# Conditioning matmuls of a hybrid decoder step: four units share one K tile, and one set of transposes per vector

## The chip, the cores and the metric

The kernel runs on one core of one Trainium2 chip. The metric is the time of one execution on the device in microseconds (us), as the median over runs; lower is better. In the profile PE is TensorE (PEld its weight loads), ACT is ScalarE, DVE is VectorE, POOL is GpSimd and SP is SyncE, which issues the transfers.

## The reference, cut to what matters

One step of a two-layer decoder trunk for 256 prompt tokens and 8 sequences of 4 tokens, 288 columns in all, at model width 2048. Layer 0 mixes with a causal convolution of 31 taps and a gated linear attention, layer 1 with a spatial gating unit and windowed attention; each has an input projection, an output projection and a SwiGLU block. All sub-layers are modulated by a conditioning vector, and that part the change touches:

```python
def adaln(c, w, b):
    return jnp.split(jax.nn.silu(c) @ w + b, 6, axis=-1)     # c: 9 rows of 2048, w: 2048 x 12288 for each layer

def modulate(x, g, shift, scale):
    return rms_norm(x, g) * (1.0 + scale[:, None, :]) + shift[:, None, :]

mp = adaln(c_prompt, w_ada[layer], b_ada[layer])             # shift, scale, gate of the mixer; the same of the FFN
hp = modulate(yp, g_mix[layer], mp[0], mp[1])
yp = yp + mp[2][:, None, :] * (op @ w_out[layer])
yp = swiglu_sublayer(yp, mp[3], mp[4], mp[5], ...)
```

So there are 12 vectors of 2048 entries (6 for each layer), each for 9 conditioning rows, and their weights are 192 MB of float32, read once.

## The kernel before

**The projections.** All activations lie with the model dimension on the partitions. A weight step is a tile of 2048 KB (`raw`, two slots, the projections and the gate/up matrices `gu`) or of 1408 KB (the down matrices, `down`). ACT rounds it to `w_hi` (L868), DVE subtracts to get `w_lo` (L1191), and PE multiplies hi by hi, lo by hi and hi by lo (L556 to L558): 48 matmuls of 288 columns for half a step, 33 for half a `down` step. A *body* is two steps, four halves. SP loads a step when the tile two steps before has been split. Semaphores order all of it.

**The conditioning work.** The 12 x 2048 columns are cut in 48 *units* of 512 columns. The weights of a unit come in four *slots* of 1024 KB, each holding four K tiles of 128 rows with 512 columns. The first 8 units (`PRE`) run at the start, before anything else can, from the four slots that `raw` gives (`load_pre`, L391); the others ride in the bodies of layer 0 with a ring `aring` of two slots (`load_ada`, L383): one unit per body. For a slot PE issues four matmuls, one into each group of 32 output columns of the array (L572): group j takes K tile 4s+j. So after four slots the four groups each hold a partial sum over four K tiles. ACT copies the bank to `adarow` (`ada_copy`, L936); PE multiplies it by `sel`, a matrix of stacked identities, four times (`ada_turn`, L582), which sums the four groups and turns the result; DVE adds the bias into `mods` (`ada_bias`, L1289). In a body the slots stand so: slot 0 after the first half, slot 1 after the second, slots 2 and 3 after the third, the turn after the fourth.

**Order of the stages.** Start (units 0 to 7), norm of x, `zr`, `gate` (4 bodies, units 8 to 11), `zconv` (4, units 12 to 15), `z` (2, units 16 and 17), the mixer `mix0`, `out` (4, units 18 to 21), norm, `gu` (11, units 22 to 32), `down` (8, units 33 to 40), `gu` (11, the first 7 with units 41 to 47), `down` (8, without units), norm; then layer 1, which has no conditioning work. Bodies of one kind run in a loop on each engine (`Fori`), with addresses from registers; the first and the last body of a segment are partly written out (`peel`).

**The convolution.** In `gate` and `zconv` DVE runs two instructions for each of 31 taps and each of 8 tiles (`conv`, L1278 and L1280) between its splits. It reads 30 history rows, which SP loads (L472, eight transfers in runs of 120 bytes) after the norm has released the memory; at the end of the first norm DVE waits for that history, and the next split of weights stands behind that wait:

```python
                    norm(norms, final=norms == 4)
                    norms += 1
                    if norms == 1:
                        dve.wait_ge(history_landed, 16 * CT)
                        dve.wait_ge(history_zero, 1)
```

SP issues the history (L472) before the weights of the second `gate` step and the first slots of unit 8.

**mix0** waits until the new convolution state has been stored (L413, eight transfers in runs of 120 bytes), which SP issues after the last load of `z`.

Of the kernel before, what the change touches and what calls it, by code (L numbers as in the profile page):

```python
# [63 lines left out]
class Seg:  # L64


    def __init__(self, kind, layer, bodies, m, first, unit=None, group=0):
        self.kind, self.layer, self.bodies, self.m = kind, layer, bodies, m
        self.first = first
        self.unit = unit  # L70
# [11 lines left out]
def plan():  # L82
    segs, norm = [], "norm"
    segs += [Seg("zr", 0, 1, 1, 0), Seg("gate", 0, 4, 2, 0, 8), Seg("zconv", 0, 4, 2, 8, 12, 0),
             Seg("z", 0, 2, 2, 16, 16, 16)]
    segs += ["mix0", Seg("out", 0, 4, 2, 0, 18), norm]
    for layer in range(2):
        if layer:
            segs += [Seg("kv", 1, 1, 1, 0), Seg("q", 1, 2, 2, 1), Seg("sgu", 1, 4, 2, 5), "mix1",
                     Seg("out", 1, 4, 2, 0), norm]  # L90
        segs += [Seg("gu", layer, 11, 2, 0, None if layer else 22),
                 Seg("down", layer, 8, 2, 0, None if layer else 33, 0)]
        if layer:
            segs += [Seg("gu", 1, 11, 2, 22)]
        else:
            segs += [Seg("gu", 0, 7, 2, 22, 41), Seg("gu", 0, 4, 2, 36)]
        segs += [Seg("down", layer, 8, 2, 16, None, 1), norm]
    return segs
# [24 lines left out]
for _s in SEGS:  # L123
# [3 lines left out]
    _s.peel = int(_s.bodies == 2 or _s.opens or _s.kind == "out")  # L127
# [9 lines left out]
GLA_A = 4 * 18  # L137


def lin(i, per, c):  # L140

    return c if i is None else i * per + c
# [31 lines left out]
def build(nc, t, o):  # L174

    ctx = ExitStack()
    with ctx:
# [29 lines left out]
        sel = sb("sel", [P, S9])  # L207
# [127 lines left out]
        def unit_uses(u):  # L335

            return lin(u[0], 4, 4 * (u[1] - PRE) + (HEADS if u[1] >= 18 else 0))

        def first_unit(u):
            return u[0] is None and u[1] == 0  # L340

        def unit_no(u):
            return lin(u[0], 1, u[1])
# [25 lines left out]
        def _(sp):  # L369
# [8 lines left out]
            def load_ada(u, s):  # L378

                if not (u[0] is None and u[1] == PRE and s < 2):  # L380
                    sp.wait_ge(ada_used, unit_no(u) * 4 + (s - 1))
                rows = t["w_ada"][bass.ds(unit_no(u) * 4 + s, 1)]
                sp.dma_start(aring[:, s % 2, :], rows.rearrange("a p n -> p (a n)")) \  # L383
                    .then_inc(ada_landed[s % 2], 16)

            def load_pre(u, s):

                if not first_unit(u):
                    sp.wait_ge(ada_used, unit_no(u) * 4 + (s - 3))
                rows = t["w_ada"][bass.ds(unit_no(u) * 4 + s, 1)]  # L390
                sp.dma_start(pre_slot(s), rows.rearrange("a p n -> p (a n)")).then_inc(cond_w_landed[s], 16)  # L391

            def body(seg, i, base, last=False):

                for j, (n, par, ls) in enumerate(steps_of(seg, i, base)):
# [8 lines left out]
                    if seg.unit is not None:  # L404
                        load_ada((i, seg.unit + base), 2 * j)
                        load_ada((i, seg.unit + base), 2 * j + 1)
# [43 lines left out]
            for s in range(4):  # L450
                load_pre((None, 0), s)
            sp.dma_start(x[:], t["xT"]).then_inc(x_landed, 16)
            with sp.Fori(0, PRE - 1) as i:
                for s in range(4):
                    load_pre((i, 1), s)
            sp.wait_ge(ada_used, 4 * PRE - 3)
            load_step(SEGS[0], 0, 0, 0)
            for seg, after in zip(PLAN, PLAN[1:] + [None]):
# [6 lines left out]
                elif seg != "norm":  # L465
# [12 lines left out]
                    if seg.peel:  # L478
                        body(seg, None, 0)
# [56 lines left out]
        def _(pe):  # L536
# [24 lines left out]
            def ada_slot(u, s, pre=False):  # L561

                if pre:
                    slot = pre_slot(s)
                    pe.wait_ge(cond_w_landed[s], unit_no(u) * 16 + 16)
                else:
                    slot = aring[:, s % 2, :]
# [1163 lines left out]
```

## Time and profile before

| | before |
|---|---|
| median of 3 runs | 3024.14 us (3020.37 to 3024.21) |
| profiled execution, its span | 3025.1 us |
| PE busy | 2829.3 us, 94% |
| DVE, ACT busy | 1414.4 us (47%), 1177.5 us (39%) |
| slot matmuls L572, busy | 163.0 us (1280 passes from `aring`), 50.9 us (256 from `raw`) |
| turns L582, busy | 50.6 us (384 passes) |
| moved by DMA | 602.59 MB, mean 199 GB/s |

A float32 matmul is recorded as two passes, so L572 has 8 records for a slot, and L582 has 8 for a turn. The profiled execution's own time is its span, 1.0 us above the median of the runs. The stages lie in the trace at: start 0 to 97 us, norm and `zr` to 133, `gate` to 262, `zconv` to 386, `z` to 458, `mix0` to 592, `out` to 718, `gu` 742 to 1074, `down` to 1261, `gu` to 1584, `down` to 1726, layer 1 after that.

### The profile page before, as it was taken

Reading aid. Unit: us, or ns where it says so; the run is one execution under the profiler, and the core shown is the slowest. Engines: PE = TensorE matmul, PEld = TensorE weight load, DVE = VectorE, ACT = ScalarE, POOL = GpSimd, SP = SyncE. Lnnn points to the kernel's source line nnn. Section 1 sums busy time; section 2 is a strip of 40 time slices with the busy share of each in tenths; the row PEclk is TensorE's granted clock in tenths of the full one; section 3 lists DMA queues with packets and bytes.
Section 4 is the critical chain, followed back from the end, with each engine's and each line's share of the span. In section 5 each row is a group of like instructions: output and inputs, shape, how many; then the busy total and the mean of one; then the engine's idle time right before and its main releaser. Section 6 shows DMA issues by size and latency. Waiting matters only on the chain.

```text
span 3025.1 us, 50764 instructions
## 1 busy us (share of the span) xinstructions
PE 2829.3 (94%) x20229; PEld 2570.6 (85%) x20229; DVE 1414.4 (47%) x2017; ACT 1177.5 (39%) x1508; POOL 79.0 (3%) x108
## 2 busy tenths in 40 slices
PE   5699995898999999999999899889899999999997
PEld 1488884687888888888999899669799999999997
DVE  0399945434443433344444535534545544444443
ACT  1333344234444332333443435433444433444433
POOL 1000000010000000000000000001000000000000
PEclk7699996599999999999999999669999999999999
DMA  9767757375777677877534444114344434444343
GB/s 383 254 259 270 279 223 84 118 273 203 272 272 283 255 281 307 318 266 272 206 132 171 151 164 158 50 60 154 125 166 166 158 135 179 167 166 166 141 155 124
DMA packets 83601, 602.59 MB, mean 199 GB/s; under 512 B 29301, under 2 KB 30645, under 8 KB 31938
## 3 DMA queue, kind: packets, MB, share of 16 engines
q1 hardware_dynamic: 83522, 601.54, 54.4%
q8 instruction: 50, 0.82, 0.1%
q14 instruction: 29, 0.24, 0.0%
HBM read 592.01 MB, written 9.49 MB: 199 GB/s over the span
## 4 chain that ended last, share of the span: by engine, by line
PE 85%; DVE 4%; ACT 4%; DMA 3%; issue 3%; SPq 1%; DVEq 0%; POOL 0%; ACTq 0%; POOLq 0%
PE ps L556 25%; PE ps L557 24%; PE ps L558 24%; PE ps L572 5%; DMA raw<-in_w_ada 3%; DVE w_lo L1191 1%; DVE cacc L1280 1%; ACT tn L1013 1%; PE ps L702 1%; PE ps L582 1%; ACT w_hi L868 1%; PE ps L741 1%; SPq L413 1%; ACT act_hi L1020 1%; PE ps L721 0%
## 5 line engine op out<-in xcount | busy, mean ns | idle before, releaser
L1191 DVE TENSOR_TENSOR w_lo<-raw,w_hi 128x2048 fp32r<-128x2048 f32 (+2 forms) x404 | 838.1, 2075 | 1172.4 <-ACT w_hi L868 1160.5
L556 PE MATMUL ps<-act_hi,w_hi 128*128 128x288 f32 x4400 | 1323.6, 301 | 64.4 <-DVE act_lo L1363 40.7
L557 PE MATMUL ps<-act_hi,w_lo 128*128 128x288 f32 x4400 | 1304.1, 296 | 0.0
L558 PE MATMUL ps<-act_lo,w_hi 128*128 128x288 f32 x4400 | 1299.0, 295 | 0.0
L868 ACT ACTIVATE w_hi<-raw 128x2048 fp32r<-128x2048 f32 (+2 forms) x404 | 702.2, 1739 | 1123.7 <-PE ps L558 1120.7
L556 PEld LDWEIGHTS ps<-act_hi,w_hi 128*128 128x128 f32 x4400 | 830.3, 189 | 154.3 <-issue 117.3
L558 PEld LDWEIGHTS ps<-act_lo,w_hi 128*128 128x128 f32 x4400 | 834.3, 190 | 0.0
L557 PEld LDWEIGHTS ps<-act_hi,w_lo 128*128 128x128 f32 x4400 | 832.3, 189 | 0.0
L556 PE MATMUL ps<-hid_hi,w_hi 128*128 128x288 f32 x1408 | 421.6, 299 | 8.5 <-DVE w_lo L1191 8.5
L558 PE MATMUL ps<-hid_lo,w_hi 128*128 128x288 f32 x1408 | 419.8, 298 | 0.0
L557 PE MATMUL ps<-hid_hi,w_lo 128*128 128x288 f32 x1408 | 419.8, 298 | 0.0
L556 PEld LDWEIGHTS ps<-hid_hi,w_hi 128*128 128x128 f32 x1408 | 267.8, 190 | 29.4 <-issue 19.3
L557 PEld LDWEIGHTS ps<-hid_hi,w_lo 128*128 128x128 f32 x1408 | 266.9, 190 | 0.0
L558 PEld LDWEIGHTS ps<-hid_lo,w_hi 128*128 128x128 f32 x1408 | 266.1, 189 | 0.0
L572 PE MATMUL ps<-aring,cond 128*32 128x512 f32 x1280 | 163.0, 603 | 1.8 <-DMA aring<-in_w_ada 1.8
L1280 DVE SCALAR_TENSOR_TENSOR cacc<-uext,vec,cacc 128x256 f32<-128x256 f32 x464 | 143.6, 364 | 3.9 <-DVE cacc L1280 1.0
L911 ACT ACTIVATE sg<-sg 128x288 f32<-128x288 f32 x96 | 42.7, 444 | 153.6 <-DVE sg L1226 153.6
L930 ACT ACTIVATE sqb<-x 128x288 f32 (+1 forms) x64 | 28.5, 445 | 143.6 <-DVE x L1210 142.5
L514 POOL TENSOR_TENSOR ssq<-ssq,sqb 128x288 f32<-128x288 f32 x89 | 71.9, 808 | 469.8 <-ACT sqb L930 401.9
L572 PE MATMUL ps<-raw,cond 128*32 128x512 f32 x256 | 50.9, 901 | 31.8 <-DMA raw<-in_w_ada 31.7
L914 ACT ACTIVATE hid_hi<-prod 128x288 f32 (+1 forms) x88 | 39.1, 445 | 100.2 <-DVE prod L1237 100.2
L1240 DVE TENSOR_TENSOR hid_lo<-prod,hid_hi 128x288 f32 (+1 forms) x88 | 40.4, 459 | 62.7 <-ACT hid_hi L914 62.7
(239 smaller groups left out, 1357.1 us busy)
## 6 DMA issues: line engine op xcount, KB each, us to landing
raw<-in_w_gu SPq DMA_DIRECT2D x88, 2048.0 KB, 7.7
aring<-in_w_ada SPq DMA_DIRECT2D x160, 1024.0 KB, 7.0
raw<-in_w_dn SPq DMA_DIRECT2D x64, 1408.0 KB, 6.0
raw<-in_w_ab SPq DMA_DIRECT2D x20, 2048.0 KB, 7.8
raw<-in_w_ada SPq DMA_DIRECT2D x32, 1024.0 KB, 8.3
raw<-in_w_out SPq DMA_DIRECT2D x16, 2048.0 KB, 7.9
raw<-in_w_cd SPq DMA_DIRECT2D x13, 2048.0 KB, 7.8
aring<-in_state_glaT SPq DMA_DIRECT2D x4, 1024.0 KB, 9.9
```

The lines of the kernel that those rows point to most:

```text
L413: sp.dma_start(o["conv_s"][:, j], rows_s(j)[:, :, TS:SW]).then_inc(conv_stored, 16)
L514: pool.tensor_tensor(ssq[:], ssq[:], sqb[:, (q + k) % 2], ALU.add).then_inc(sq_added, 1)
L556: pe.matmul(bank, w_hi[:, h, cols], hi[:, kt, :], start=begin, stop=False)
L557: pe.matmul(bank, w_lo[:, h, cols], hi[:, kt, :], start=False, stop=False)
L558: mm = pe.matmul(bank, w_hi[:, h, cols], lo[:, kt, :], start=False, stop=end)
L572: mm = pe.matmul(ps[32 * j:32 * j + 32, ADA_BANK, :], cond[:, 4 * s + j, :], slot[:, j * ADA_N:(j + 1) * ADA_N], start=(s == 0), stop=(s = ...
L868: act.activation(w_hi[:, h, 0:w], raw[:, par, h * w:(h + 1) * w], ACT.Copy).then_inc(hi_done, 1)
L911: act.activation(sg[:, 0], sg[:, 0], ACT.Exp).then_inc(sig_ready, 1)
L914: act.activation(at(hid_hi, ls + seg.first % BLK), prod[:], ACT.Copy).then_inc(hid_hi_done, 1)
L1191: dve.tensor_tensor(w_lo[:, h, 0:w], raw[:, par, h * w:(h + 1) * w], w_hi[:, h, 0:w].bitcast(F32), ALU.subtract).then_inc(split_done, 1)
L1240: dve.tensor_tensor(at(hid_lo, j), prod[:], at(hid_hi, j).bitcast(F32), ALU.subtract) \
L1280: ins = dve.scalar_tensor_tensor(out, row, wk, acc, ALU.mult, ALU.add)
```

## The change

The unit of work on the conditioning becomes a *group* g = 4v + part: vector v, of which a group takes four units (2048 columns) and four of the 16 K tiles. Slot j of a group holds one K tile for the four units, so column group u of the array takes unit u and all four use the same stationary tile `cond[:, 4*part+j, :]`. The sum over K runs on in the bank over the 16 slots of a vector. The copy, the turn and the bias happen once per vector (12 times in all, not 48), and the turn is four transposes. `sel` is gone. The layout of `w_ada` in memory stays, so a slot is read in runs of 2 KB (4 per partition, from four places 4 MB apart) where it was read in rows of 8 KB.

Groups 0 to 7 run at the start, 8 to 11 in `gate`, 12 to 15 in `zconv`, none in `z`, 16 to 19 in `out`, 20 to 27 in the first 8 bodies of `gu`, 28 to 35 in `down`, 36 to 43 in the first 8 bodies of the second `gu`, 44 to 47 in the first 4 bodies of the second `down`. In all of these but `down`, slots 0 and 1 stand together after the first half. Segments that carry groups are written out in full on every engine (no loop). The wait for the history moves to the first tap of the first tile.

```diff
-        segs += [Seg("gu", layer, 11, 2, 0, None if layer else 22),
-                 Seg("down", layer, 8, 2, 0, None if layer else 33, 0)]
...
+        ada = [(None, 0)] * 4 if layer else [(20, 8), (28, 8), (36, 8), (44, 4)]
+        segs += [Seg("gu", layer, 11, 2, 0, *ada[0]), Seg("down", layer, 8, 2, 0, *ada[1]),
+                 Seg("gu", layer, 11, 2, 22, *ada[2]), Seg("down", layer, 8, 2, 16, *ada[3], group=1), norm]
...
-    _s.peel = int(_s.bodies == 2 or _s.opens or _s.kind == "out")
+    _s.peel = int(_s.bodies == 2 or _s.opens or _s.kind == "out") if _s.unit is None else _s.bodies - 1
...
+        def ada_rows_of(g, j):
+            v, part = divmod(g, 4)
+            rows = t["w_ada"].rearrange("(v u s) p n -> v s p u n", u=4, s=4)[v, part]
+            return rows[:, :, j * ADA_N:(j + 1) * ADA_N]
...
-            sp.dma_start(sel[:], t["sel"]).then_inc(consts_landed, 16)
...
-                for j in range(4):
-                    mm = pe.matmul(ps[32 * j:32 * j + 32, ADA_BANK, :], cond[:, 4 * s + j, :],
-                                   slot[:, j * ADA_N:(j + 1) * ADA_N], start=(s == 0), stop=(s == 3))
+                for u in range(4):
+                    mm = pe.matmul(ps[32 * u:32 * u + 32, ADA_BANK, :], cond[:, 4 * part + j, :],
+                                   slot[:, u * ADA_N:(u + 1) * ADA_N], start=(part == 0 and j == 0),
+                                   stop=(part == 3 and j == 3))
...
-            def ada_turn(u):
-                pe.wait_ge(ada_rows, unit_no(u) + 1)
...
-                    mm = pe.matmul(ps[:, SEL_BANK, 16 * q:16 * q + S9], adarow[:, q * P:(q + 1) * P], sel[:],
-                                   start=True, stop=True)
+            def ada_turn(g):
+                v, part = divmod(g, 4)
+                if part < 3:
+                    return
+                pe.wait_ge(ada_rows, v + 1)
...
+                    mm = pe.transpose(ps[:, SEL_BANK, q * P:(q + 1) * P], adarow[:, q * P:(q + 1) * P], ident[:])
...
-                    if u and j == 0:
-                        ada_slot(u, 0)
+                    if g is not None and j == 0:
+                        ada_slot(g, 0)
+                        if paired_slots:
+                            ada_slot(g, 1)
...
-                        pe.wait_ge(ada_biased, 18)
+                        pe.wait_ge(ada_biased, 4)
...
-            ada_copy((None, 0))
             act.wait_ge(x_landed, 16)
-            squares_of_x(0)
-            with act.Fori(0, PRE - 1) as i:
-                ada_copy((i, 1))
-                squares_of_x(2 * i + 2)
+            for g in range(PRE):
+                squares_of_x(2 * g)
+                ada_copy(g)
...
                 if 0 in taps:
-                    if not (isinstance(j, int) and j == 0):
+                    if isinstance(j, int) and j == 0:
+                        dve.wait_ge(history_landed, 16 * CT)
+                        dve.wait_ge(history_zero, 1)
+                    else:
                         dve.wait_ge(conv_ready, j)
...
-                    if norms == 1:
-                        dve.wait_ge(history_landed, 16 * CT)
-                        dve.wait_ge(history_zero, 1)
```

## Rows read from the trace of the kernel before

**Rows 1.** The page: PE's granted clock in 40 slices; instruction fetches, their MB and share.

```profile
PEclk7699996599999999999999999669999999999999
...
q8 instruction: 50, 0.82, 0.1%
```

**Rows 2.** Busy time by stretch: from:to us, length, busy time of each engine, clock, DMA.

```profile
126.30:136.50 10.20, 3.14 (x13) 3.15 (x14) 4.49 (x2) 0.00 (x0) 0.00 (x0) 0.50 1.10 313
166.10:262.20 96.10, 93.17 (x697) 82.03 (x697) 90.15 (x224) 33.93 (x40) 0.00 (x0) 1.00 0.66 251
262.20:385.70 123.50, 123.50 (x929) 109.06 (x930) 117.15 (x283) 38.69 (x39) 0.00 (x0) 1.00 0.73 280
742.00:1074.00 332.00, 332.00 (x2497) 293.15 (x2494) 135.47 (x137) 133.06 (x160) 0.00 (x0) 1.00 0.71 268
1480.00:1584.00 104.00, 104.00 (x783) 104.00 (x781) 50.09 (x53) 46.09 (x58) 0.00 (x0) 1.00 0.41 149
```

**Rows 3.** Timeline of PE in one `zconv` body: start, length, line, operation.

```profile
268.50 0.29 PE L558 MATMUL ps<-act_lo,w_hi 128*128 128x288 f32 x1
269.72 0.40 PE L556 MATMUL ps<-act_hi,w_hi 128*128 128x288 f32 x1
...
283.66 0.29 PE L558 MATMUL ps<-act_lo,w_hi 128*128 128x288 f32 x1
285.74 0.40 PE L556 MATMUL ps<-act_hi,w_hi 128*128 128x288 f32 x1
...
292.11 0.29 PE L558 MATMUL ps<-act_lo,w_hi 128*128 128x288 f32 x1
293.05 0.38 PE L556 MATMUL ps<-act_hi,w_hi 128*128 128x288 f32 x1
```

**Rows 4.** Timeline of PE at four transposes in layer 1, full clock.

```profile
2012.24 0.66 PE L803 MATMUL ps<-ident,free_hi 128*128 128x128 f32 x4
```

**Rows 5.** Timeline of PE: the last slots and the last turn of the start.

```profile
93.66 1.93 PE L572 MATMUL ps<-raw,cond 128*32 128x512 f32 x8 [0.56 <-DMA raw<-in_w_ada]
96.17 1.94 PE L572 MATMUL ps<-raw,cond 128*32 128x512 f32 x8 [0.57 <-DMA raw<-in_w_ada]
98.82 1.88 PE L582 MATMUL ps<-sel,adarow 128*128 128x9 f32 x8 [0.72 <-ACT adarow L936]
```

**Rows 6.** By stretch, DMA share and GB/s last: 8 KB rows, 120 bytes, 2 KB twice.

```profile
40.00:80.00 40.00, 28.00 (x160) 8.64 (x156) 0.59 (x3) 5.03 (x12) 6.35 (x8) 0.71 1.00 406
123.50:130.00 6.50, 0.00 (x0) 0.00 (x0) 0.00 (x0) 0.11 (x1) 0.00 (x0) 0.72 1.29 178
1750.60:1751.60 1.00, 1.00 (x10) 1.00 (x9) 0.94 (x1) 0.03 (x1) 0.00 (x0) 1.00 0.81 250
1750.80:1751.40 0.60, 0.60 (x7) 0.60 (x6) 0.60 (x1) 0.00 (x0) 0.00 (x0) 1.00 0.60 214
```

**Rows 7.** PE at the history wait and the second half; the first two slot loads in `gate`.

```profile
133.36 0.61 PE L556 MATMUL ps<-act_hi,w_hi 128*128 128x288 f32 x1 [12.04 <-DVE w_lo L1191]
...
142.37 0.40 PE L556 MATMUL ps<-act_hi,w_hi 128*128 128x288 f32 x1
...
L383 SPq DMA_DIRECT2D aring<-in_w_ada x2: 432/432/432, 128.8 to 129.3; - x2
...
DMA to landing us min/median/max: 10.1/11.1/12.1
```

**Rows 8.** Timeline of `gate`: taps in a written-out body and in the loop; PE's next step.

```profile
155.33 8.47 DVE L1280 SCALAR_TENSOR_TENSOR cacc<-uext,vec,cacc 128x256 f32<-128x256 f32 x30
214.21 4.65 DVE L1280 SCALAR_TENSOR_TENSOR cacc<-uext,vec,cacc 128x256 f32<-128x256 f32 x14
166.06 0.40 PE L556 MATMUL ps<-act_hi,w_hi 128*128 128x288 f32 x1 [0.21 <-DVE w_lo L1191]
```

**Rows 9.** PE in `z` at the sum of squares; a weight load of slot 3 in `down`.

```profile
432.37 0.75 PE L592 MATMUL ps<-ssq,ones 128*128 128x288 f32 x2 [3.98 <-POOL ssq L514]
...
1139.51 0.13 PEld L572 LDWEIGHTS ps<-aring,cond 128*32 128x32 f32 x4 [0.33 <-DMA aring<-in_w_ada]
```

More of the change, by code:

```diff
@@ L64, with __init__ @@
 class Seg:
-    def __init__(self, kind, layer, bodies, m, first, unit=None, group=0):
+    def __init__(self, kind, layer, bodies, m, first, unit=None, units=0, group=0):
         self.kind, self.layer, self.bodies, self.m = kind, layer, bodies, m
         self.first = first
-        self.unit = unit
+        self.unit, self.units = unit, units
         self.group = group
@@ L83, in plan @@
     segs, norm = [], "norm"
-    segs += [Seg("zr", 0, 1, 1, 0), Seg("gate", 0, 4, 2, 0, 8), Seg("zconv", 0, 4, 2, 8, 12, 0),
-             Seg("z", 0, 2, 2, 16, 16, 16)]
-    segs += ["mix0", Seg("out", 0, 4, 2, 0, 18), norm]
+    segs += [Seg("zr", 0, 1, 1, 0), Seg("gate", 0, 4, 2, 0, 8, 4), Seg("zconv", 0, 4, 2, 8, 12, 4),
+             Seg("z", 0, 2, 2, 16, group=16)]
+    segs += ["mix0", Seg("out", 0, 4, 2, 0, 16, 4), norm]
     for layer in range(2):
@@ L136 @@
 NORM_STATS = [1, 3, 4, 6, 7]
-GLA_A = 4 * 18
+GLA_A = 4 * 16
 def lin(i, per, c):
@@ L477, in _ @@
                             sp.dma_start(place[:], t[name]).then_inc(mix1_consts, 16)
-                    if seg.peel:
-                        body(seg, None, 0)
+                    for b in range(seg.peel):
+                        body(seg, None, b)
                     turns = seg.bodies - 1 - seg.peel
@@ L605, in body @@
                 for j, (n, par, ls) in enumerate(steps_of(seg, i, base)):
-                    u = None if seg.unit is None else (i, seg.unit + base)
+                    g = group_of(seg, base)
+                    paired_slots = seg.kind != "down"
                     half(seg, n, par, 0, first and j == 0, hidden if j == 0 else None)
@@ L849, in _ @@
                 if seg.bodies > start:
-                    if seg.bodies - start > 1:
+                    if seg.unit is not None:
+                        for b in range(start, seg.bodies):
+                            body(seg, None, b)
+                    elif seg.bodies - start > 1:
                         with pe.Fori(0, seg.bodies - start) as i:
@@ L977, in body @@
                         split(nxt, n + 1, 1 - par, 0)
-                    if seg.unit is not None and j == 1:
-                        ada_copy((i, seg.unit + base))
+                    g = group_of(seg, base)
+                    if g is not None and j == 1:
+                        ada_copy(g)
                     if seg.kind == "z" and ls == 2:
@@ L1171, in _ @@
                 else:
-                    if seg.peel:
-                        body(seg, None, 0)
+                    for b in range(seg.peel):
+                        body(seg, None, b)
                     turns = seg.bodies - 1 - seg.peel
@@ L1321, in body @@
                         split_lo(nxt, n + 1, 1 - par, 1)
-                    if seg.unit is not None and j == 1:
-                        ada_bias((i, seg.unit + base))
+                    g = group_of(seg, base)
+                    if g is not None and j == 1:
+                        ada_bias(g)
                     if convolves and opening and j == 0:
@@ L1592, in _ @@
             dve.tensor_tensor(cond[:, :, 0:S9], cond[:, :, 0:S9], cols, ALU.mult).then_inc(cond_ready, 1)
-            dve.wait_ge(consts_landed, 48)
-            ada_bias((None, 0))
-            with dve.Fori(0, PRE - 1) as i:
-                ada_bias((i, 1))
+            dve.wait_ge(consts_landed, 32)
+            for g in range(PRE):
+                ada_bias(g)
             split_lo(SEGS[0], 0, 0, 0)
@@ L1612, in _ @@
                 else:
-                    if seg.peel:
-                        body(seg, None, 0)
+                    for b in range(seg.peel):
+                        body(seg, None, b)
                     turns = seg.bodies - 1 - seg.peel
```

131 lines of the change are left out of this document (64 added, 67 removed).

## The prediction

> **What bounds the kernel now.** I read the page first, then the busy time by stretch, then the timeline of PE. PE's clock is at its upper level nearly everywhere but at the start, in the mixers and at the norms [rows 1]. In the stages of layer 0 that carry the conditioning, PE is busy for the whole stretch: 123.50 of 123.50 us in `zconv`, 332.00 of 332.00 in the first `gu` [rows 2]. So there each microsecond of PE's work is a microsecond of the kernel. Three places are different. At the start the DMA share is 1.00 and slots arrive 2.51 us apart, with PE idle before each [rows 5, 6]. In `gate` DVE is busy 90.15 of 96.10 us beside PE's 93.17 [rows 2]. And `mix0` waits for its state store.
>
> **What conditioning costs PE in a body.** A half-step matmul takes 104.00/783 = 0.133 us where nothing is between [rows 2], so a bare body of 192 is 25.5 us and a bare `down` body of 132 is 17.5. The gaps, as start of the last matmul before to start of the first one after, less 0.13, plus 0.11 by which that first one is longer (0.40 for 0.29): one slot alone 1.22, so 1.20 us; two slots together 2.08, so 2.06; a turn 0.94, so 0.90 [rows 3]. A body with a unit is then 25.5 + 2 x 1.20 + 2.06 + 0.90 = 30.86 us; `zconv` has four in 123.50, 30.88 each [rows 2]. A `down` body is 22.9.
>
> **The change part by part.**
>
> *Turns.* 40 turns behind the start go (36 us of PE). 10 come, each four transposes: one such set shows 0.66 us [rows 4], where the 8 passes with `sel` show 1.88 at the lower clock [rows 5] and so 0.94 at the upper; 0.90 - 0.28 = 0.6 each. The copies and bias adds that go, on ACT and DVE, lie beside PE's matmuls and are costed at nothing outside `gate`.
>
> *Slots.* Their number stays, and four column groups run side by side as now. Where two single slots become a pair, a body saves 2 x 1.20 - 2.06 = 0.34 us. A body with a group is then 29.62 us.
>
> *Stages where PE is the bound*, with the new places of the groups and turns. `zconv`: 4 x (29.62 - 30.86) + 0.6 = -4.4. `out`: the same, -4.4. First `gu`: 11 x 30.86 = 339.5 becomes 8 x 29.62 + 3 x 25.5 + 2 x 0.6 = 314.7, so -24.8. First `down`: 8 x -0.90 + 2 x 0.6 = -6.0. Second `gu`: 7 x 30.86 + 4 x 25.5 = 318.0 becomes 314.7, so -3.3. Second `down`, bare now, gets four groups at 2 x 1.20 + 2.06 and a turn: +18.4.
>
> *`z`.* Two units leave. Not all of it is gained: at 432.37 PE waits 3.98 us for the sum of squares [rows 9], and that chain starts when the second step's last half ends. Ahead of this point lie two single slots and one pair, 4.4 us, and the chain to the state store moves by as much. What leaves behind it would only lengthen a wait. So -4.4.
>
> *Reads of 2 KB.* The trace has no large transfer of them. Transfers of 8 KB rows at share 1.00 move 406 GB/s, 323 ns a row on each of 16 engines; runs of 120 bytes move 178 at share 1.29, so 138 GB/s and 13.9 ns [rows 6]. A straight line through the two is 9.3 ns plus 0.0383 ns a byte: 88 ns for 2 KB, 351 for four, 1.086 times the 323. A slot then takes 2.73 us for 2.51, 0.22 more. From below: nothing. From above: the stretch with a 256 KB load of 2 KB rows, mixed with smaller ones, moves 250 GB/s at share 0.81, so 309 at full share, 1.31 times as long or 0.78 us a slot; a narrower stretch gives 214/0.60 = 357, 0.34 a slot [rows 6]. I take 0.22, as the two ends of the line are the cleaner rows. At the start 31 slots are in sequence: 31 x 0.22 = +6.7 us. In `gu`, `out` and `zconv` slots have time (DMA share 0.71 to 0.73 [rows 2]). In `down` the slot 3 load lands just as PE wants it, a weight load there waits 0.33 us for it [rows 9], so 12 bodies x 0.22 = +2.6: 1.8 in the first `down`, 0.9 in the second.
>
> The Trainium skill ("DMA: Bandwidth & Descriptors", section "Why small descriptors are slow (HBM only)") gives a fixed cost of some 3 cycles for each descriptor, beside one cycle for each 32 bytes. An estimate from it is 4 x 67 cycles for 259, 1.035 times as long, and with it the start would lose 2.7 us where my line says 6.7.
>
> *The end of the start.* The last turn took 1.88 us at the lower clock [rows 5]; half of the passes, -1.0. The start in all: +5.7.
>
> *History wait.* It holds PE for 12.04 us, until 133.36 [rows 7]. Moved, it lets PE start soon after it came free at 133.4 - 12.0 = 121.3, at about 122 (the first split still has to end); so at first sight -11. But slots 0 and 1 of the first group now stand together after that first half. They are issued at 128.8 and 129.3, behind the history in SP's queue, which the change leaves there, and land 10.1 and 12.1 us later, at 138.9 and 141.4 [rows 7]. With 0.2 and 0.4 for the 2 KB runs, PE ends its half at 122 + 48 x 0.133 + a little = 128.7, waits, and begins the second half at about 143.0, where it began at 142.4 [rows 7]. What is late next is that slot pair, and PE's rest of some 10 us comes with a clock at the lower level, as the rest before 133 did (0.50 over 126.3 to 136.5 [rows 2]): matmuls at half speed for a few us, +2. The following half step needs DVE's split after 32 tap instructions (8.47 us for 30) with PE waiting 0.21 [rows 8]; that chain stays, and the slot that stood ahead of it no longer helps. So the second step pair begins 2.7 us later than 166.1.
>
> *Loops written out.* In the `gate` loop 14 tap instructions take 4.65 us, 0.33 each; written out 30 take 8.47, 0.28 [rows 8]. The stretch from 166.1 has three bodies, two of them in the loop; written out they save DVE 2 x 62 x 0.05 = 6.2 of its 90.15 us, so 28.0 a body, and with its waits, (96.1 - 90.15)/3 = 2.0, 30.0 beside PE's 29.6. Three bodies are then 90.0 where 96.1 went [rows 2], and a turn: -5.5. `gate` in all: +2.7 - 5.5 = -2.8. From both sides: -11 if the pair doesn't wait, +3 if the loop gains nothing.
>
> *Sum:* +5.7 (start) - 2.8 (`gate`) - 4.4 (`zconv`) - 4.4 (`z`) - 4.4 (`out`) - 24.8 (`gu`) - 4.2 (`down`) - 3.3 (`gu`) + 19.3 (`down`) = -23.3 us. Against the profiled span of 3025.1 that is 3001.8, and the median of the runs lies 1.0 below the span: 3001 us.
>
> **The rivals.**
>
> *The 2 KB reads are dear* (ends on the other side). Without them the sum is -32.6. They count 31 + 12 = 43 times, so they decide from 32.6/43 = 0.76 us a slot, 3.3 us for 2.51. At the upper row, 0.78, the time is 3024.1 - 32.6 + 33.5 = 3025. For it: no row shows a long transfer of this kind, and the four sources lie 4 MB apart. Against it: the narrower stretch gives 0.34, which is 3006.
>
> *The reads run at half rate.* The four places of a slot 4 MB apart could fall on the same part of the memory. If a slot took 5.0 us for 2.5: start +77; a `down` body would move 2 x 1408 KB (7.1 us at 406 GB/s) and four slots, 27.0 us for PE's 22.0, so 12 x 5 = +60; `gu`-like bodies 10.3 + 20 = 30.3 for 29.6, +15. Time 3024 - 33 + 152 = 3143. The trace has no such pattern for or against. The Trainium skill ("DMA: Bandwidth & Descriptors", section "Latency and other measured facts", the row on HBM row pitch) reports copies whose partitions lie 4 MiB apart at about half the rate; here only the four units do, partitions lie 8 KB apart as before, and that is why it gets a small chance.
>
> *The history gain is kept.* If the slots land earlier or the pair's wait is short, -10 more: 2991. Against it stand the two landing times.
>
> *The written-out code costs.* Instructions come in 50 fetches of 16 KB now [rows 1]; some 40 bodies more of code may add 80. If each stopped PE 0.5 us: +40, 3041. Against it: `z` is written out already and shows no wait of that kind.
>
> **How the numbers follow.** Chances: forecast 0.66; history gain kept 0.08; dear reads 0.12, half of them within 0.2%; half rate 0.07; code 0.07. A measurement of this kernel can tell about 0.2%, 6 us. Faster is 0.66 + 0.08 = 0.74, same 0.10 (with a little of the code case), slower 0.16. The forecast's own range is 2992 (reads free) to 3012 (0.34 a slot and some us in `gate`). The range to hold 8 in 10 goes from 2990 to 3027, the dear reads and 2 us of scatter included; half rate and most of the code case stay out.
>
> **What would show it.** L582 gone, 48 transposes in its place. Bodies of `zconv` and `gu` at 29.6 us, of `gu` without a group at 25.5. Slots at the start 2.7 us apart; from 3.2 on the forecast is wrong. PE beginning `gate` near 128 (122 plus the longer start) and then waiting about 10 us for `aring`, not for `w_lo`. The wait of 3.98 us in `z` a little longer, the state store 4.4 us nearer to the end of `zconv`. The second `down` 19 us longer. Waits for `aring` in `down`, over 0.5 us a body, would be the term I trust least.

## The result

The changed kernel takes 3126.07 us (median of 4 runs, 3123.63 to 3129.25) where the kernel before takes 3024.18 (4 runs, 3020.37 to 3025.53): 1.034 times as long, 95% interval 1.033 to 1.036. Forecast were 3001 us and a range up to 3027. The change was to save some 23 us and costs 102. The profiled execution has a span of 3121.9 us and a time of 3123.63. In every kernel measured from here on an execution's time lies about 1.7 us above its span, so that of the kernel before, with its span of 3025.1, was a somewhat long one (some 3027 us for the median of 3024); this matters for the table by stage below.

### The profile after

The page of the changed kernel: its granted clock, the rate of its transfers and the instruction fetches, beside [rows 1]; then the chain that ended last, by line, and how long loads of conditioning weights took from issue to landing (last number).

```profile
PEclk7589996599999989899999999958999999999999
...
DMA packets 157248, 603.58 MB, mean 193 GB/s; under 512 B 29157, under 2 KB 30501, under 8 KB 130098
...
q8 instruction: 108, 1.77, 0.2%
...
PE ps L553 23%; PE ps L555 22%; PE ps L554 22%; DMA aring<-in_w_ada 10%; PE ps L570 5%; DMA raw<-in_w_ada 3%; ACT tn L1021 1%; PE ps L706 1%; DVE w_lo L1197 1%; ACT w_hi L872 1%; PE ps L745 1%; SPq L412 1%; ACT act_hi L1028 1%; PE ps L737 0%; POOL ssq L511 0%
...
aring<-in_w_ada SPq DMA_DIRECT2D x160, 1024.0 KB, 10.3
...
raw<-in_w_ada SPq DMA_DIRECT2D x32, 1024.0 KB, 12.3
```

The loads of `w_ada` into `aring` are 10% of the chain that sets the end. In the list of PE's waits the two loads of conditioning weights come first (us in total, times, longest):

```profile
PE ps L570 <- DMA aring<-in_w_ada: 89.0, 27, 13.8
PE ps L570 <- DMA raw<-in_w_ada: 66.4, 31, 12.1
```

The same two waits in the kernel before add up to 1.8 and 31.7 us. Together they grew by 121.9 us, more than the 102 that the kernel lost: it is TensorE's waits for the conditioning weights that cost the time, and the places show where. At the start (timeline of PE) the slots come at irregular distances:

```profile
27.15 1.94 PE L570 MATMUL ps<-raw,cond 128*32 128x512 f32 x8 [4.10 <-DMA raw<-in_w_ada]
35.27 1.94 PE L570 MATMUL ps<-raw,cond 128*32 128x512 f32 x8 [6.18 <-DMA raw<-in_w_ada]
37.94 1.94 PE L570 MATMUL ps<-raw,cond 128*32 128x512 f32 x8 [0.73 <-DMA raw<-in_w_ada]
40.51 1.62 PE L570 MATMUL ps<-raw,cond 128*32 128x512 f32 x8 [0.64 <-DMA raw<-in_w_ada]
44.74 1.63 PE L570 MATMUL ps<-raw,cond 128*32 128x512 f32 x8 [2.60 <-DMA raw<-in_w_ada]
...
126.31 1.93 PE L570 MATMUL ps<-raw,cond 128*32 128x512 f32 x8 [4.28 <-DMA raw<-in_w_ada]
```

The last slot begins at 126.31 where it began at 96.17 [rows 5]. In the first `down` stage (1084.63 to 1317.51) slot 3, right behind slot 2, waits for its load in each of the eight bodies, 3.94 to 5.49 us, 35.8 in all:

```profile
1109.30 1.24 PE L570 MATMUL ps<-aring,cond 128*32 128x512 f32 x8 [4.45 <-DMA aring<-in_w_ada]
...
1137.06 1.68 PE L570 MATMUL ps<-aring,cond 128*32 128x512 f32 x8 [4.15 <-DMA aring<-in_w_ada]
...
1158.89 0.29 PE L554 MATMUL ps<-hid_hi,w_lo 128*128 128x288 f32 x1
...
1165.65 1.93 PE L570 MATMUL ps<-aring,cond 128*32 128x512 f32 x8 [4.94 <-DMA aring<-in_w_ada]
1167.52 0.61 PE L553 MATMUL ps<-hid_hi,w_hi 128*128 128x288 f32 x1
1167.92 0.44 PE L554 MATMUL ps<-hid_hi,w_lo 128*128 128x288 f32 x1
```

The same matmul is recorded with 0.29 us ahead of such a wait and 0.44 behind it: the granted clock is 1.00 over 1155 to 1159 us and 0.50, its lower level, over 1166 to 1169.

By stretch (start, first `down`, second `down`; clock, DMA share and GB/s last):

```profile
30.00:90.00 60.00, 32.75 (x144) 4.26 (x148) 0.31 (x1) 7.34 (x17) 12.32 (x16) 0.65 0.98 317
1084.63:1317.51 232.88, 194.83 (x1322) 158.88 (x1321) 63.62 (x84) 47.97 (x40) 0.00 (x0) 0.91 0.85 254
1636.06:1826.81 190.75, 166.73 (x1191) 147.51 (x1189) 64.17 (x85) 55.41 (x55) 12.54 (x16) 0.95 0.69 213
```

At the start the DMA engines are as busy as before (0.98 for 1.00) and move 317 GB/s where they moved 406 [rows 6]. A share near 1 tells that the engines are occupied, not that they move much. In `gate` and `out` the timeline has waits for `aring` too. The one of 13.81 us at the first pair is mostly the wait that the prediction had put there (11.15 us of it stand in the kernel with whole rows, below); the second and third rows are new:

```profile
171.76 1.93 PE L570 MATMUL ps<-aring,cond 128*32 128x512 f32 x8 [13.81 <-DMA aring<-in_w_ada]
...
178.50 1.94 PE L570 MATMUL ps<-aring,cond 128*32 128x512 f32 x8 [4.82 <-DMA aring<-in_w_ada]
...
634.04 1.94 PE L570 MATMUL ps<-aring,cond 128*32 128x512 f32 x8 [5.82 <-DMA aring<-in_w_ada]
```

### The profile page after: what moved, and what is told of

Read it like the earlier page. It is cut to its first block, busy times and chain, and to the rows that moved or that the text cites. A ratio compares the mean times of both kernels' runs of the same rounds, so it can differ in the third digit from the quotient of the medians.

```text
span 3121.9 us, 47038 instructions
## 1 busy us (share of the span) xinstructions
PE 2814.6 (90%) x19893; PEld 2540.3 (81%) x19893; DVE 1397.9 (45%) x1981; ACT 1155.9 (37%) x1472; POOL 78.6 (3%) x108
## 3 DMA queue, kind: packets, MB, share of 16 engines
q8 instruction: 108, 1.77, 0.2%
## 4 chain that ended last, share of the span: by engine, by line
PE 77%; DMA 13%; ACT 4%; DVE 3%; issue 2%; SPq 1%; POOL 0%; ACTq 0%; POOLq 0%; DVEq 0%
PE ps L553 23%; PE ps L555 22%; PE ps L554 22%; DMA aring<-in_w_ada 10%; PE ps L570 5%; DMA raw<-in_w_ada 3%; ACT tn L1021 1%; PE ps L706 1%; DVE w_lo L1197 1%; ACT w_hi L872 1%; PE ps L745 1%; SPq L412 1%; ACT act_hi L1028 1%; PE ps L737 0%; POOL ssq L511 0%
## 5 line engine op out<-in xcount | busy, mean ns | idle before, releaser
L553 PE MATMUL ps<-hid_hi,w_hi 128*128 128x288 f32 x1408 | 430.3, 306 | 8.9 <-DVE w_lo L1197 8.9
L554 PEld LDWEIGHTS ps<-hid_hi,w_lo 128*128 128x128 f32 x1408 | 277.1, 197 | 0.0
L555 PEld LDWEIGHTS ps<-hid_lo,w_hi 128*128 128x128 f32 x1408 | 272.4, 193 | 0.0
L570 PE MATMUL ps<-aring,cond 128*32 128x512 f32 x1280 | 172.5, 636 | 89.1 <-DMA aring<-in_w_ada 89.0
L570 PEld LDWEIGHTS ps<-aring,cond 128*32 128x32 f32 x1280 | 29.6, 110 | 154.4 <-DMA aring<-in_w_ada 121.6
L1289 DVE SCALAR_TENSOR_TENSOR cacc<-uext,vec,cacc 128x256 f32<-128x256 f32 x464 | 132.1, 360 | 0.0
L570 PE MATMUL ps<-raw,cond 128*32 128x512 f32 x256 | 60.1, 1031 | 66.4 <-DMA raw<-in_w_ada 66.4
L570 PEld LDWEIGHTS ps<-raw,cond 128*32 128x32 f32 x256 | 6.4, 138 | 117.0 <-DMA raw<-in_w_ada 104.5
L934 ACT ACTIVATE sqb<-x 128x288 f32<-128x288 f32 (+1 forms) x64 | 28.5, 445 | 141.1 <-DVE x L1216 139.5
```

What stands on the lines that cost most here:

```text
L553: pe.matmul(bank, w_hi[:, h, cols], hi[:, kt, :], start=begin, stop=False)
L554: pe.matmul(bank, w_lo[:, h, cols], hi[:, kt, :], start=False, stop=False)
L555: mm = pe.matmul(bank, w_hi[:, h, cols], lo[:, kt, :], start=False, stop=end)
L570: mm = pe.matmul(ps[32 * u:32 * u + 32, ADA_BANK, :], cond[:, 4 * part + j, :], slot[:, u * ADA_N:(u + 1) * ADA_N], start=(part == 0 and j ...
L1289: ins = dve.scalar_tensor_tensor(out, row, wk, acc, ALU.mult, ALU.add)
```

## The experiments

Two things could make the loads slow, and the change brought both: runs of 2 KB where 8 KB were, and a pattern of places in memory. A slot is now read as 512 runs: from each of four units' blocks (4 MB apart), from each of 128 rows (8 KB apart), one quarter. The next slot takes the next quarter of the same rows. The experiments lay `w_ada` out in other ways, all prepared with the inputs; the kernel's own work stays.

### First round: size or place

**Whole rows.** A slot's 8 KB for one partition stand in one row.

```diff
-            v, part = divmod(g, 4)
-            rows = t["w_ada"].rearrange("(v u s) p n -> v s p u n", u=4, s=4)[v, part]
-            return rows[:, :, j * ADA_N:(j + 1) * ADA_N]
+            return t["w_ada"][4 * g + j].rearrange("p (u n) -> p u n", n=ADA_N)
...
-    f["w_ada"] = a["w_ada"].reshape(2, 4, 4, P, UNITS, ADA_N).transpose(0, 4, 1, 3, 2, 5).reshape(8 * UNITS, P, 4 * ADA_N)
+    f["w_ada"] = a["w_ada"].reshape(2, 4, 4, P, 6, 4, ADA_N).transpose(0, 4, 1, 2, 3, 5, 6).reshape(8 * UNITS, P, 4 * ADA_N)
```

> Edit: the changed kernel, with w_ada laid out in memory so that a slot is one block of 1 MB with rows of 8 KB (one K tile, four units side by side). All else as changed. Theory A (the reads are what costs; the rest of the change does what the sum said): slots at the start about 2.5 us apart again, no waits of 4 us in the down bodies, time 3024 - 32 or so, 2985 to 3000. Rival C (something else in the change costs the 100 us: written-out code, the pairing of slots, the order of loads): time stays over 3060.

Measured: 2989.39 us, 0.989 of before (0.988 to 0.991). The rest of the change does what it was forecast to do, and the loads are the whole trouble.

**Dense blocks of 2 KB runs.** A slot is one block of 1 MB with four parts of 256 KB, one for each unit, with rows of 2 KB (`reshape(8 * UNITS, 4, P, ADA_N)`, read as `"u p n -> p u n"`).

> Edit: the changed kernel, w_ada laid out so that a slot is one block of 1 MB, but as four sub-blocks of 256 KB, one for each unit, with rows of 2 KB. So the transfer still consists of runs of 2 KB (512 of them), but they lie close together and use every byte of the block. Theory A (the place of the runs in memory costs, not their size): near the straight line of the prediction, slots 2.7 us apart, time 2995 to 3010. Rival B (runs of 2 KB as such cost it, wherever they lie): as the changed kernel, 3110 to 3140, slots 3.7 us apart on average.

Measured: 3002.66 us, 0.994 (0.991 to 0.996). Runs of 2 KB by themselves cost some 13 us (the four runs lie between 2997 and 3011), near the 9 of the prediction. In the stretch 30 to 90 us they move 382 GB/s where whole rows move 415, so 2.74 us a slot for 2.53: 0.22 us more, as the prediction had it. They are not the cause.

**Units 24 KB further apart.** Each unit's block gets 24 KB of padding; rows and quarters as in the change.

```diff
-            rows = t["w_ada"].rearrange("(v u s) p n -> v s p u n", u=4, s=4)[v, part]
-            return rows[:, :, j * ADA_N:(j + 1) * ADA_N]
+            rows = t["w_ada"].rearrange("(v u) x -> v u x", u=4)[v, :, part * P * 4 * ADA_N:(part + 1) * P * 4 * ADA_N]
+            return rows.rearrange("u (p n) -> p u n", n=4 * ADA_N)[:, :, j * ADA_N:(j + 1) * ADA_N]
...
-    f["w_ada"] = a["w_ada"].reshape(2, 4, 4, P, UNITS, ADA_N).transpose(0, 4, 1, 3, 2, 5).reshape(8 * UNITS, P, 4 * ADA_N)
+    f["w_ada"] = a["w_ada"].reshape(2, 4, 4, P, UNITS, ADA_N).transpose(0, 4, 1, 3, 2, 5).reshape(2 * UNITS, -1)
+    f["w_ada"] = np.pad(f["w_ada"], ((0, 0), (0, 6144)))
```

> Edit: the changed kernel, with 24 KB of padding behind each unit in w_ada, so that the four units of a slot lie 4 MB + 24 KB apart and no longer at a power of two; a slot still takes only 2 KB out of each row of 8 KB. Theory A1 (the 4 MB between the units costs): time falls to 2995 to 3030. Theory A2 (reading one quarter of each 8 KB row costs) and rival B: no change, 3110 to 3140.

Measured: 3102.09 us, 1.027 (1.025 to 1.029). Of the 123 us by which the change lies above the dense blocks (3126.07 less 3002.66), 24 go; the exact distance of 4 MB is not by itself the main cause.

**Dense rows, units still 4 MB apart.** Within a unit each K tile is one block of 256 KB, so the 128 rows of a read lie one behind the other.

```diff
-            rows = t["w_ada"].rearrange("(v u s) p n -> v s p u n", u=4, s=4)[v, part]
-            return rows[:, :, j * ADA_N:(j + 1) * ADA_N]
+            return t["w_ada"].rearrange("(v u) k p n -> v k p u n", u=4)[v, 4 * part + j]
...
-    f["w_ada"] = a["w_ada"].reshape(2, 4, 4, P, UNITS, ADA_N).transpose(0, 4, 1, 3, 2, 5).reshape(8 * UNITS, P, 4 * ADA_N)
+    f["w_ada"] = a["w_ada"].reshape(2, 4, 4, P, UNITS, ADA_N).transpose(0, 4, 1, 2, 3, 5).reshape(2 * UNITS, 16, P, ADA_N)
```

> Edit: the changed kernel, w_ada laid out unit by unit, 4 MB each, and in a unit slot by slot with rows of 2 KB: so the four runs of a partition lie exactly 4 MB apart as in the changed kernel, but the 128 partitions of a unit form one dense block of 256 KB, where the changed kernel takes 2 KB of each 8 KB. Theory A2 (the quarter rows): time falls to 2995 to 3030. Theory A1 (the 4 MB): stays at 3110 to 3140. Rival B: stays too.

Measured: 3003.97 us, 0.994 (0.992 to 0.995), like the dense blocks. Of those 123 us 122 or so hang on one thing: whether the runs of a read are neighbours or each the same quarter of an 8 KB row.

### Second round: which pattern

Either every run lies at the same place within 8 KB, or a run without its neighbours is dear as such. Padding tells these apart, as it keeps the runs apart but moves them.

**Rows 10 KB apart** (2 KB of padding behind each row):

```diff
+    f["w_ada"] = np.pad(f["w_ada"], ((0, 0), (0, 0), (0, ADA_N)))
```

> As the changed kernel, but each 8 KB row of w_ada stands at a pitch of 10 KB (2 KB of padding behind it), so the 2 KB that a slot reads of each row fall in turn on all four quarters of an 8 KB stretch, and still only one 2 KB piece in 10 KB is read. Theory P (reads are dear when all 512 of a slot lie at the same place within 8 KB): the time comes to that of the dense blocks, about 3003 us. Theory S (reads are dear because each stands alone, its neighbours unread): 3100 to 3126 us stays.

**Units 2 KB further apart** (the padding of 24 KB above, with 2 KB):

> As the changed kernel, but the units stand 4 MB and 2 KB apart, so the four units' reads of one slot fall on four different quarters of 8 KB; within a unit every read is still at the same quarter of each 8 KB. Theory P: about 3003 us, if it is the slot as a whole that has to be spread. Theory S: 3100 to 3126 us. Between them (about 3060 us) if what counts is the spread within what one transfer has under way at a time.

Measured: 2998.14 us (0.994, 0.992 to 0.995) and 2999.3 (0.993, 0.991 to 0.994). In both, a run stands alone and costs no more than in the dense blocks. 2 KB behind each unit take away all that 24 KB left.

**Units 4 KB further apart**, two places of four:

> As the changed kernel, but the units stand 4 MB and 4 KB apart, so that the 2 KB reads of one slot fall on two of the four quarters of an 8 KB stretch, where the changed kernel has one and the kernel with 2 KB behind each unit has four (2999 us). If the cost of a read goes with how many of a slot's reads share a place within 8 KB, the time lies between: about 3020 to 3060 us. Rival (two places do already, all or nothing): 2997 to 3004 us; rival (places 4 KB apart count as the same): 3100 to 3126 us.

Measured: 3011.59 us, 0.997 (0.995 to 0.998): between one place and four, but nearer to four than I had expected.

**Rows 16 KB apart, and 12 KB apart** (padding of `4 * ADA_N` and `2 * ADA_N` behind each row):

> As the changed kernel, but each 8 KB row of w_ada stands at a pitch of 16 KB, so that all reads of a slot are at one place in 16 KB instead of 8 KB. If only the place within 8 KB counts: 3100 to 3130 us, as the changed kernel. If the pattern that collides is longer than 8 KB, the reads collide more: above 3140 us. If a slot's four K tiles read in turn are what makes it dear (their rows are neighbours in memory), it falls: below 3090 us.

> As the changed kernel, but each 8 KB row stands at a pitch of 12 KB, so that the reads of neighbouring partitions alternate between two places 4 KB apart within 8 KB, inside each unit, with the units all alike. If it counts how many of a slot's reads share a place within 8 KB, wherever they are in the slot: about 3012 us, as with the units 4 KB apart. If the pattern is longer than 8 KB, the reads spread over more places than two: 2997 to 3003 us. If a spread over the partitions is worth less than one over the units: 3030 to 3110 us.

Measured: 16 KB apart 3036.72 us, 1.005 (1.003 to 1.007); 12 KB apart 3001.17, 0.993 (0.991 to 0.994). The first falls below the 3090 of its third case, but not for the reason given there: the K tiles of a group stand as quarters of the same rows with 2 KB or 10 KB as well, and those kernels take 2999.3 and 2998.1. Neither of the two cases that counted places came. All its runs share one place within 8 KB, and yet nearly three quarters of the place's cost are gone (3036.7 and 3126.1 above the 3002.7 of dense blocks). With 12 KB, two places shared out over the partitions did as well as four. The padding to 16 KB had changed two distances, of the rows and of the units, so one more run changed the units' alone, to 8 MB:

> As the changed kernel, rows at their pitch of 8 KB, but the units 8 MB apart instead of 4 MB, as they are in the kernel whose rows stand 16 KB apart (3037 us against 3126). If it was the units' distance that helped there: about 3037 us here. If it was the rows' pitch: 3100 to 3130 us here.

Measured: 3147.87 us, 1.042 (1.039 to 1.046). The units' distance did not help; the rows' did. Here are all patterns, with the rate in the stretch 30 to 90 us, where hardly any other load runs, and PE's waits for `aring`:

| runs | rows apart | units apart | GB/s at the start | waits for `aring`, us | us |
|---|---|---|---|---|---|
| 8 KB | 8 KB | (one row) | 415 | 15.6 | 2989.4 |
| 2 KB | 10 KB | 5 MB | 387 | 17.3 | 2998.1 |
| 2 KB | 8 KB | 4 MB + 2 KB | 387 | 18.0 | 2999.3 |
| 2 KB | 12 KB | 6 MB | 384 | 19.5 | 3001.2 |
| 2 KB | 2 KB | 256 KB | 382 | 17.9 | 3002.7 |
| 2 KB | 2 KB | 4 MB | 378 | 22.4 | 3004.0 |
| 2 KB | 8 KB | 4 MB + 4 KB | 374 | 28.3 | 3011.6 |
| 2 KB | 16 KB | 8 MB | 345 | 37.1 | 3036.7 |
| 2 KB | 8 KB | 4 MB + 24 KB | 321 | 71.9 | 3102.1 |
| 2 KB | 8 KB | 4 MB (the change) | 317 | 89.0 | 3126.1 |
| 2 KB | 8 KB | 8 MB | 314 | 105.1 | 3147.9 |

The runs come from several sets, in which the kernel before took 3020.5 to 3024.2 us, so differences of 2 or 3 us between lines are not read.

The change and the kernel with whole rows differ only in the layout of `w_ada`, so in the size and the place of the runs. Their rows of the same stages, start, first and second `down`, read best side by side; this is the kernel with whole rows:

```profile
30.00:90.00 60.00, 39.06 (x200) 5.29 (x196) 0.31 (x1) 3.92 (x9) 7.38 (x10) 0.70 1.01 415
1028.78:1213.74 184.96, 179.87 (x1323) 149.76 (x1321) 63.64 (x84) 47.98 (x40) 0.00 (x0) 0.98 0.83 317
1529.03:1692.02 162.99, 158.28 (x1191) 143.27 (x1189) 64.18 (x85) 55.41 (x55) 12.54 (x16) 1.00 0.65 245
```

In the first `down` the same matmuls (1322 and 1323 recorded) fill 194.83 us in the change and 179.87 here. So of the 47.9 us between the two, 33.0 are PE's idle time and 15.0 its slower pace: the granted clock is 0.91 for 0.98, and the rows at 1158.89 to 1167.92 above show the lower level right behind a wait. In the second `down` it is 19.3 and 8.5 of 27.8.

### The other steps of the prediction

**The first pair's loads ahead of the history** (and ahead of SP's wait for the end of the norm), on the kernel with whole rows:

```diff
                     if seg.kind == "gate":
+                        load_ada(PRE, 0)
+                        load_ada(PRE, 1)
                         sp.wait_ge(act_ready, KT)
...
-                    if g is not None:
+                    if g is not None and not (g == PRE and j == 0):
```

> The kernel with whole 8 KB rows (2989 us), with the loads of the first group's slots 0 and 1 issued ahead of the six constants and the eight history loads instead of behind them. By the prediction's step for the gate stage (the slot pair takes the place of the history wait because it stands behind these loads in SP's queue) the 11.2 us wait of the first pair goes, and 6 to 11 us with it: 2979 to 2983 us. Rival: the weights behind the history loads are as late, or the constants are, and hold TensorE instead: 2987 to 2990 us.

Measured: 2980.98 us, 0.987 (0.985 to 0.989), 8.4 less than with whole rows alone, and 7.0 less than the 2988.0 of the next run, which stems from the same set. It is the fastest kernel of this study. The timeline of PE with whole rows shows the wait of the first pair:

```profile
117.87 0.40 PE L551 MATMUL ps<-act_hi,w_hi 128*128 128x288 f32 x1 [0.81 <-DVE w_lo L1195]
135.68 1.93 PE L568 MATMUL ps<-aring,cond 128*32 128x512 f32 x8 [11.15 <-DMA aring<-in_w_ada]
```

With the loads ahead it is gone, and part of it comes back one step later as a wait for DVE's split (what makes that late was not taken apart):

```profile
119.15 0.40 PE L553 MATMUL ps<-act_hi,w_hi 128*128 128x288 f32 x1 [0.81 <-DVE w_lo L1197]
125.74 1.92 PE L570 MATMUL ps<-aring,cond 128*32 128x512 f32 x16
139.35 0.58 PE L553 MATMUL ps<-act_hi,w_hi 128*128 128x288 f32 x1 [5.09 <-DVE w_lo L1197]
```

**The history wait put back** into its old place, on the kernel with whole rows (and taken out at the first tap):

```diff
                     norms += 1
+                    if norms == 1:
+                        dve.wait_ge(history_landed, 16 * CT)
+                        dve.wait_ge(history_zero, 1)
```

> The kernel with whole 8 KB rows (2989 us), with the history wait back in its old place ahead of the first split of the gate stage. By the prediction's step the slot pair waits for about the same moment, so the move of the history wait is worth little here: 2989 to 2992 us. Rival, that the history gain was kept: 2998 to 3001 us.

Measured: 2988.0 us, 0.989 (0.988 to 0.991), not to be told from 2989.4.

**The history wait alone moved**, on the kernel before (the reverse of this edit):

> The kernel before, with the history wait alone moved from ahead of the gate stage's first split to the first convolution tap; nothing else of the change. By the prediction's step the first half of gate starts up to 12 us sooner, and the single slot that follows it still waits for a load that stands behind the history in the queue, to about 138.9 us: most of the 12.0 us comes back as that wait, 2 to 4 us remain: 3016 to 3018 us against 3020 to 3021 before. Rival (the history gain is kept): 3009 to 3012 us.

Measured: 3021.11 us beside 3022.01 of before, 0.9995 (0.9986 to 1.0005), so between -4 and +2 us. The medians lie 0.9 apart where I expected 2 to 4, and the trace shows the size in place: from the first half step to the second body of `gate` it is 55.5 us (164.21 less 108.72), 56.0 before. The timeline of that kernel shows the wait that takes the place of the 12.04 us of [rows 7], and the start of the second body, where DVE holds PE as in [rows 8]:

```profile
120.79 0.40 PE L556 MATMUL ps<-act_hi,w_hi 128*128 128x288 f32 x1 [0.80 <-DVE w_lo L1191]
137.36 1.93 PE L572 MATMUL ps<-aring,cond 128*32 128x512 f32 x8 [9.90 <-DMA aring<-in_w_ada]
164.21 0.40 PE L556 MATMUL ps<-act_hi,w_hi 128*128 128x288 f32 x1 [0.21 <-DVE w_lo L1191]
```

**The loops alone written out**, on the kernel before:

```diff
-    _s.peel = int(_s.bodies == 2 or _s.opens or _s.kind == "out")
+    _s.peel = int(_s.bodies == 2 or _s.opens or _s.kind == "out") if _s.unit is None else _s.bodies - 1
...
-                    if seg.peel:
-                        body(seg, None, 0)
+                    for b in range(seg.peel):
+                        body(seg, None, b)
...
```

> The kernel before, with the loops over bodies of the conditioning stages written out on all engines and nothing else changed. The prediction's terms for written-out loops (5.5 us in gate, whose turns each lost an issue gap, and little elsewhere) give 3013 to 3018 us. Rival (written-out code costs instruction loading): 3022 to 3036 us.

Measured: 3021.3 us, 0.9995 (0.9986 to 1.0005): between -4 and +2 us. In its trace PE goes from the second body of `gate` (162.21) to `zconv` (254.86) in 92.7 us where before took 96.1 [rows 2], so 3.4 us came and 5.5 were forecast. Up to the sum of squares in `z` they are kept: from the first half step (106.08) to there (425.06) it is 318.98 us, 322.33 before. The time of the whole kernel is too blunt to show 3.4 us.

**Slots 0 and 1 apart again** in all stages, on the kernel with whole rows (`paired_slots = False`):

> The kernel with whole 8 KB rows (2989 us), with slot 1 back behind the second half of the first step, as before the change, in all stages and not only in the down stages. The prediction gave the pairing no cost and no gain beyond the first pair of gate: 2986 to 2992 us. Rival (the pair saves a change between slot and body each time, 23 bodies by 0.1 to 0.3 us): 2991 to 2996 us.

Measured: 2995.77 us, 0.991 (0.989 to 0.992), 6.4 above the paired one. My expectation misstated the prediction, which had priced the pair: 0.34 us a body, in 28 bodies 9.5. The two times alone don't settle it, as their intervals overlap (0.989 to 0.992 and 0.988 to 0.991) and stages whose code is the same in both differ by -3.9 us (first `down`) and +2.6 (second). The timelines do: a body of `zconv` takes 30.01 us apart (260.80 to 290.81) and 29.69 paired (261.05 to 290.74), so 0.32 for 0.34.

## Why the prediction was wrong

**The step that failed is "Reads of 2 KB".** It took the price of a read from the size of its run, by a line between runs of 120 bytes and rows of 8 KB, 0.22 us a slot. That line was good for what it measures: dense runs of 2 KB cost 13.3 us in all (3002.66 less 2989.39) where the terms say 9.3. But it priced a run by its size alone, and the reads of the change have a place besides a size, one quarter of each 8 KB row in all 128 rows of all four units, and the place costs 123.4 us more. By stage, each from its first matmul to that of the next, in us more or less than in the profiled execution of the kernel before:

| stretch | predicted | the change | with whole rows | predicted without the 2 KB terms |
|---|---|---|---|---|
| to the first half step | +5.7 | +29.2 | -4.3 | -1.0 |
| `zr`, `gate`, `zconv`, `z` to the sum of squares | -11.6 | -0.9 | -12.1 | -11.6 |
| to the end of `mix0` | 0 | -1.4 | -0.7 | 0 |
| `out` | -4.4 | +5.7 | -4.1 | -4.4 |
| norm | 0 | +0.1 | +0.1 | 0 |
| first `gu` | -24.8 | -22.4 | -24.5 | -24.8 |
| first `down` | -4.2 | +46.2 | -1.7 | -6.0 |
| second `gu` | -3.3 | -0.1 | -3.4 | -3.3 |
| second `down` | +19.3 | +42.9 | +15.1 | +18.4 |
| layer 1 | 0 | -2.4 | -2.2 | 0 |
| sum | -23.3 | +96.8 | -37.8 | -32.7 |

The last column sets against the measured one what the rest of the prediction was worth. As the profiled execution of the kernel before was a long one, the sum of -37.8 is too large: by the medians of one set whole rows gain 31.2 us (3020.54 to 2989.39), and 32.7 were forecast without the reads of 2 KB.

**The bounds.** The upper one, 0.78 us a slot, came from a stretch with one load of 256 KB in it. Against the whole rows, the start lost 33.4 us on 31 slots, 1.08 each, and the two `down` stages 47.9 and 27.8 us on 32 and 16 slots, 1.5 and 1.7 each. In `down` the prediction named the right place, slot 3, and charged it for one read a body, 12 times 0.22. But slot 3's waits there, 35.8 us in eight bodies, are 4.5 us each, which is four times the 1.08 that a slot loses at the start. So it seems that what all four slots of a body lose comes out in that one wait, at a DMA share of 0.83 with whole rows; the clock adds to it. The number of reads that count was too small as well as their price. The prediction's own sign came true: slots 3.2 us apart or more would tell that it is wrong, and 317 GB/s is 3.3 us a slot.

**The rivals.** The half rate (3143 us, chance 0.07) came nearest in time, through a mechanism that the runs refute in the form I gave it. Units 4 MB apart with dense rows take 3003.97 us; units moved off that distance by 24 KB take 3102. My reason for the small chance was that the partitions lie 8 KB apart "as before". They do, but before a read took the whole 8 KB and now a quarter. And the rate fell to 317 of 415 GB/s, not to half. The Trainium skill ("DMA: Bandwidth & Descriptors", section "Latency and other measured facts", the row on HBM row pitch) says that copies ran at about half the rate when the rows of the partitions lay 4 MiB apart, and that 4 KiB more between them restored it. No run here has partitions that far apart; here the slow reads have them 8 KB apart and only the units 4 MB. The cure agrees, behind each row (12 KB apart, 3001.2 us for 3126.1) and behind each unit (3011.6). But the runs show more than it says: 2 KB behind each unit did better, and 24 KB, three times the row, did little.

**What held.** *Turns and slots:* first `gu` -24.5 for -24.8, `out` -4.1 for -4.4 in the kernel with whole rows. Two successive pairs in its first `gu` stand 14.85 us apart, so a body is 29.70 us; I had 29.62. A turn takes 0.60 us. Both rows are from its timeline:

```profile
254.12 0.60 PE L582 MATMUL ps<-ident,adarow 128*128 128x128 f32 x4
...
779.43 1.92 PE L568 MATMUL ps<-aring,cond 128*32 128x512 f32 x16
794.28 1.92 PE L568 MATMUL ps<-aring,cond 128*32 128x512 f32 x16
```

*`z`:* the changed kernel's wait for the sum of squares, 3.98 us in [rows 9], became 4.84, "a little longer". *History wait:* right, and now shown from three sides. The pair waits 11.15 us for loads that stand behind the history in SP's queue; put back, the history wait costs nothing that can be told; and when the loads go ahead of it, 7 to 8 us come. *`gate`:* counted from the first half step, the second body begins 1.7 us later than before in the kernel with whole rows (163.54 less 105.79, against 166.06 less 110.04), where I had 2.7, and from there to `zconv` takes 90.9 us, where I had 90.6. *Written-out code:* 108 fetches of 1.77 MB for 50 of 0.82 [rows 1] cost nothing that these runs can tell, and the rival is out. The first `down` gained 1.7 us of 6.0 in the kernel with whole rows, in part because of waits for `aring` that stay (3.9 us outside `gate`'s first pair, 1.99 of them at 1206.38); in the three other kernels with whole rows, whose code is the same there, it gained 3.6, 4.7 and 5.6. The second grew by 15.1 for 18.4. The start is 4.3 us shorter where I said 1.0, but the kernel with only its loops written out, whose start is unchanged, also reaches its first half step 4.0 us sooner than that of [rows 5]; so this is scatter between executions.

**What stays open.** Why the memory gives less for this pattern. "The same place within 8 KB" agrees with the runs at 10 KB, 12 KB, 2 KB, 24 KB and 8 MB, and fails for rows 16 KB apart, which share that place and lose about a quarter as much. The layouts with padded rows also moved the units (to 5, 6 and 8 MB apart), and only the 8 MB were tried alone. No run here tells which part of the memory the addresses share. Nor was it tried to keep the layout and read different quarters for different units in one slot, which the column groups would allow.

## What to carry to other kernels

When an edit changes how a load walks its tensor, price three things, not one: the size of its runs, the place of all its runs relative to each other (which quarter of which rows, over partitions and over outer blocks), and in how many stages the transfers have no slack. If a load takes the same slice of each row and the rows lie as here (8 KB apart, in blocks 4 MB apart), lay the slices out densely or put a slice's length of padding behind each block; here that gave back 127 us for 2 KB a block. And a wait that is moved is worth only what the next load in the same queue lets through: here 12 us of waiting moved brought about 1 us, and issuing the next loads earlier brought 7 to 8.

## What was not expected of the hardware

- With all DMA engines busy (share 0.98 to 1.05) the rate of 1 MB loads in 2 KB runs ranged from 314 to 387 GB/s with the place of the runs alone.
- Padding of 2 KB behind each 4 MB did as much as a wholly dense layout (2999.3 and 3002.7 us), while 24 KB did little (3102.1) and another 4 MB did harm (3147.9).
- Rows 16 KB apart were 89 us faster than rows 8 KB apart (3036.7 and 3126.1), though both hold every run of a slot at one place within 8 KB.
- With waits of some 4.5 us in each `down` body PE's granted clock was 0.91 in that stage where it was 0.98 without them, and its slower pace cost another 15.0 us beside the 33.0 of idle time.
